# First attention of a two-layer encoder: PSUM copies at the end of a step, value products that wait by four key blocks, squares ahead of exponentials

## The reference, cut to what matters

```python
for qb in range(S // Q_BLOCK):                     # 8 blocks of 128 queries
    n_keys = q0 + Q_BLOCK                          # keys up to the block's end
    s = einsum('bqhcd,bkhcd->bhcqk', q[:, q0:n_keys], k[:, :n_keys]) * scale
    s = s + _rel_bias(q0, n_keys, rel_table)[None, :, None]
    p = _masked_softmax(s, _chunk_mask(q0, n_keys)[None, None, None])
    a = p[:, :, 0] - lam * p[:, :, 1]
    outs.append(einsum('bhqk,bkhe->bqhe', a, v[:, :n_keys]))
o = _rms_norm(concatenate(outs, axis=1), subln_w) * (1.0 - lam_init)
return o.reshape(B, S, D_MODEL) @ w_o
```

## Time and profile before

| | |
|---|---|
| median of the runs | 3080.66 us (3074.52, 3080.66, 3080.73) |
| the profiled execution | 3074.19 us, span of its records 3072.5 us |
| first attention in it | about 150 to 760 us |
| PE busy over the span | 2708.4 us (88%) |
| DVE, ACT, POOL busy | 1689.0 (55%), 1184.6 (39%), 336.0 us (11%) |

### The profile page before, as it was taken

The page is one execution under the profiler, slowest core; times in us unless marked ns, Lnnn a source line. Parts: engine busy times, 40 slices in busy tenths (PEclk is TensorE's granted clock), DMA queues, the critical chain, the costliest instruction groups (busy, mean ns, idle before and its releaser), DMA issues.

```text
span 3072.5 us, 37975 instructions
## 1 busy us (share of the span) xinstructions
PE 2708.4 (88%) x12716; PEld 2231.9 (73%) x12716; DVE 1689.0 (55%) x2888; ACT 1184.6 (39%) x2125; POOL 336.0 (11%) x362
## 2 busy tenths in 40 slices
PE   1678878887999999999998788888789999999996
PEld 1566666665778888888776677777567888888884
DVE  3466666665575444354375777777558323232346
ACT  0355555554262120312255565665426212131223
POOL 2000000000020001016032322222101000000000
PEclk9789998886999999999999999999899999999997
DMA  6422222223434324142233111111353211111122
GB/s 195 143 68 73 70 69 66 64 59 145 150 95 130 103 69 135 44 129 61 71 115 86 21 32 27 27 32 26 128 159 86 77 48 48 48 48 48 48 82 76
DMA packets 331200, 245.78 MB, mean 80 GB/s; under 512 B 41000, under 2 KB 303447, under 8 KB 331103
## 3 DMA queue, kind: packets, MB, share of 16 engines
q1 hardware_dynamic: 314062, 185.82, 20.7%
q0 software_dynamic: 17040, 58.73, 6.3%
HBM read 215.12 MB, written 33.59 MB: 81 GB/s over the span
## 4 chain that ended last, share of the span: by engine, by line
PE 63%; DVE 13%; ACT 10%; issue 9%; DMA 4%; ACTq 0%; DVEq 0%; POOL 0%; SPq 0%; POOLq 0%
PE PA L1651 31%; PE SC L1651 24%; PE VB L1739 3%; DVE H L1184 2%; DVE soft L1566 2%; ACT H L729 2%; ACT X L745 2%; DMA ada<-in_ada_w 1%; DVE W L1102 1%; ACT X L1028 1%; ACT W L683 1%; PE TB L1658 1%; DVE H L1223 1%; ACT H L723 1%; DVE X L1588 1%
## 5 line engine op out<-in xcount | busy, mean ns | idle before, releaser
L1651 PE MATMUL PA<-U,W 128*128 128x512 f32 x3840 | 948.8, 402 | 80.8 <-DVE W L1102 46.9
L1651 PEld LDWEIGHTS PA<-U,W 128*128 128x128 f32 x3840 | 730.6, 192 | 245.5 <-issue 57.7
L683 ACT ACTIVATE W<-raw 128x1024 fp32r<-128x1024 f32 (+2 forms) x262 | 259.8, 992 | 830.9 <-PE PA L1651 389.9
L1651 PE MATMUL SC<-U,W 128*128 128x512 f32 x2064 | 484.2, 394 | 4.4 <-DVE W L1102 4.2
L1651 PEld LDWEIGHTS SC<-U,W 128*128 128x128 f32 x2064 | 389.5, 189 | 91.5 <-DVE W L1102 5.9
L1102 DVE TENSOR_TENSOR W<-raw,W 128x1024 fp32r<-128x1024 f32 (+2 forms) x262 | 313.8, 1198 | 99.6 <-ACT W L683 97.9
L1651 PE MATMUL PA<-H,W 128*128 128x512 f32 x1536 | 358.7, 393 | 3.2 <-DVE W L1102 3.2
L1651 PE MATMUL SC<-H,W 128*128 128x512 f32 x1536 | 354.4, 390 | 0.0
L1651 PEld LDWEIGHTS PA<-H,W 128*128 128x128 f32 x1536 | 288.6, 189 | 64.3 <-DVE W L1102 3.6
L1651 PEld LDWEIGHTS SC<-H,W 128*128 128x128 f32 x1536 | 288.5, 188 | 60.5 <-issue 1.0
L729 ACT ACTIVATE H<-TB 128x512 fp32r<-128x512 f32 (+3 forms) x216 | 107.8, 499 | 217.0 <-PE TB L1658 215.6
(11 more groups left out here) (209 smaller groups left out, 2984.1 us busy)
## 6 DMA issues: line engine op xcount, KB each, us to landing
raw<-in_ffn_w SPq DMA_DIRECT2D x160, 512.0 KB, 4.1
ada<-in_ada_w POOLq DMA_DIRECT2D x96, 512.0 KB, 4.7
U<-attention_out SPq DMA_DIRECT2D x4, 3584.0 KB, 17.4
raw<-in_da_w_qkv SPq DMA_DIRECT2D x24, 512.0 KB, 4.2
attention_out<-ostage SPq DMA_DIRECT2D x32, 256.0 KB, 2.7
raw<-in_da_w_o SPq DMA_DIRECT2D x16, 512.0 KB, 4.1
X<-residual SPq DMA_DIRECT2D x4, 2048.0 KB, 11.6
attention_out<-ostage SPq DMA_DIRECT2D x64, 128.0 KB, 2.3
```

The costliest lines, as they stand in the source:

```text
L683: nc.scalar.activation(W[:, slot, 0, 0:kt * P], raw[:, slot, 0:kt * P], ACT.Copy).then_inc(w_hi, 1)
L1651: ins = mm(bank, W[:, slot, a, kt * P:(kt + 1) * P], moving(b, kt)[:, cols], start=kt == first and (a, b) == SPLIT[0], stop=kt == last and ...
```

## The change

There are three edits in the written order, and none of them adds arithmetic.

- On ACT, `copy_piece0` moves from just behind the exponentials to the end of the step, behind `scale0` and the reciprocal root. On DVE, `lo_piece0` moves behind the second evacuation group `a_lo(h, s-1, 1)`.
- On ACT, `out_square` moves ahead of the exponentials.
- On PE, `values0` waits before key block 0 for the evacuation of the blocks 0 to 3, and before key block 4 for that of the blocks 4 to 7, in place of one wait for the last group.

```diff
@@ ACT heads0
                         a_hi(h - 1, NQ - 1, 0)
+                    if square is not None:
+                        out_square(*square)
                     exps0(h, s)
-                    if s == 0 and not is_first(h):
-                        copy_piece0(p, h, LAST_PIECE)
-                    if proj and s in PIECE_DONE:
-                        copy_piece0(1 - p, h + 1, PIECE_DONE[s])
...
                     if store is not None:
                         out_hi(a0, store[0], store[1], P, ofin)
-                    if square is not None:
-                        out_square(*square)
                     scale0(h, s)
                     if square is not None:
                         rms_of_pair(*square)
+                    if s == 0 and not is_first(h):
+                        copy_piece0(p, h, LAST_PIECE)
+                    if proj and s in PIECE_DONE:
+                        copy_piece0(1 - p, h + 1, PIECE_DONE[s])
@@ DVE heads0
-                    if s == 0 and not is_first(h):
-                        lo_piece0(p, h, LAST_PIECE)
-                    if proj and s in PIECE_DONE and PIECE_DONE[s] // 2 != 1:
-                        lo_piece0(1 - p, h + 1, PIECE_DONE[s])
...
                         a_lo(h - 1, NQ - 1, 1)
+                    if s == 0 and not is_first(h):
+                        lo_piece0(p, h, LAST_PIECE)
+                    if proj and s in PIECE_DONE and PIECE_DONE[s] // 2 != 1:
+                        lo_piece0(1 - p, h + 1, PIECE_DONE[s])
@@ PE values0
-                pe.wait_ge(a0["t_evac"], 14 * h + group_of0(last, 1 if last >= 4 else 0) + 1)
                 for j in range(last + 1):
+                    if j % 4 == 0:
+                        pe.wait_ge(a0["t_evac"], 14 * h + group_of0(last, j // 4) + 1)
```

## The result

| | before | after |
|---|---|---|
| median of 20 runs each | 3074.05 us (3062.27 to 3086.77) | 3081.50 us (3078.38 to 3082.94) |
| profiled execution | 3074.19 us, span 3072.5 | 3080.43 us, span 3078.7 |
| ratio | | 1.0027, 95% interval 1.0017 to 1.0038 |

The change made the kernel slower by 0.27%. The forecast was 3080 us and "no change". The time lies 1.5 us beside it, but what it was to be compared with was 3074 and not the 3080.66 of the first three runs, and 0.27% is more than the 0.2% that I had called no change.

The account below looks back on a forecast made before the run. PE, the busiest engine, was seen held by waits and slow clock, within a step chain over DVE and ACT. Chain terms of -7.8 us plus 13.2 for the clock gave +5.4 on 3074.19: 3080 us, range 3064 to 3099.

Parts of the forecast that it names:

- no change: Whole kernel: the forecast itself, 3080 us, own range 3074 to 3087, called within 0.2% of before; chance 0.36.
- The named signs: First attention: value waits gone, L1223 and `max0` spacings, new PE waits in steps 1 and 7, heads of 76 to 79 us.
- step 1: Projection and `max0` start together, -3.3 us; with the earlier square -4.0 us a head, before the clock.
- the clock term in step 1: First half piece of the next projection, after PE's wait: low clock, 4.71 us against 3.02, +1.7 a head.
- its bound: Limits for the slowed half piece in step 1: 0 and 12 x 0.2 more matmul time, given as 2.3 us.
- The 4 us that I gave for it: Half piece of step 1 at half rate throughout, twice 12 x 0.24: total some 4 us higher.
- step 3: Scaling, root and copies in series add +2.8 us; slack of 1.5 before the exponentials is used up: net +1.3 a head.
- Step 7: Exponentials no longer behind an evacuation that waited for PE, -1.3 us; slowed second half piece, +0.5 a head.
- step 0: Copies come behind two evacuations, staging and scaling, partly offset by less waiting for PE's transposes: +0.4 us a head.
- PE takes the whole gain: Rival: DVE's step has room for the later copy, 13 us a head saved in seven heads, 2983 us; chance 0.05.
- The clock holds: Rival: PE's few instructions in the new gaps keep the clock up, the 13.2 us go, 3066 us; chance 0.25.
- The low clock spreads: Rival, steps 7 to 1: slow half pieces delay step 1's transposes, 4.0 us a head, 3090 to 3094 us; chance 0.34.

Follow-up runs that it names:

- e4: Early squares and split value wait put on the kernel before, without the late copies: ratio 0.9865, median 3029.7 us.
- e6: The full change, but ACT copies the q pieces (steps 6 and 0) early, right behind the exponentials: ratio 0.9969 to the kernel before, 3061.9 us.
- e7: The full change, but ACT copies the k pieces (steps 2, 3) early, and in fact the v pieces too: ratio 0.9937 to the kernel before, 3055.7 us.
- e9: The full change without the split wait (late copies and early squares): ratio 1.0038 to the kernel before, 3082.8 us.
- e5: The full change plus 16 overwritten filler matmuls on PE before step 1's wait for the weight slab: ratio 1.0011 to the kernel before, 3076.4 us.
- e1: Only the late copies and low parts, put on the kernel before; squares and value wait as before: ratio 1.0128, 3110.5 us.
- e10: The full change without the early squares (late copies and split wait): ratio 1.0114 to the kernel before, 3109.7 us.

## Why the prediction was wrong

**The mechanism held.** The named signs are in the profile after: of the waits before L1740 0.15 us is left; L1223 of step 6 3.41 us behind the difference (forecast about 3.4); `max0` of step 7 13.52 us behind that of step 6 (13.4); PE 4.93 us before the projection of step 1, released by DVE's W (3 to 5), and 4.10 before the scores of the next head (about 4). Heads 1, 2, 4, 5 and 6 last 78.3 to 79.3 us (76 to 79), and head 3 82.6, since DVE's pause at its end is now on the path in full (13.16 us for the 9.22 of step 7 elsewhere). e4, e6 and e7 show the cause by undoing it.

**The step that failed is the size of the clock term in step 1.** I put the slow half piece at 4.71 us, +1.7, from the nearest row, and gave 2.3 as its bound. It took 5.35 us here, and 5.17 to 5.49 in heads 1, 3, 5 and 6 as well; only in head 4 it was 4.60. The six together took 31.2 us, 2.9 more than six of 4.71. With that in place of the term, the sum is +8.3 us or 0.27%, which is not "no change". The granted clocks (the number before the last two) tell why the row was the wrong one. Shown are the row in the kernel before, the piece of head 4 in the kernel after, and a piece of e9 that had the low clock from end to end:

```profile
545.59:550.30 4.71, 4.71 (x17) 3.69 (x15) 2.73 (x9) 1.84 (x3) 0.00 (x0) 0.64 0.00 0
...
472.67:477.27 4.60, 4.60 (x14) 3.62 (x15) 1.95 (x10) 1.10 (x4) 0.00 (x0) 0.63 0.57 171
...
550.04:555.53 5.49, 5.49 (x13) 4.28 (x14) 1.95 (x10) 1.09 (x4) 0.00 (x0) 0.50 0.48 143
```

With 0.64 a part of the 4.71 ran at the full clock, while the piece of 5.35 us had 0.51 over its first 5.2 us. So that row was no measure of a piece that begins after a wait of 4.9 us, and the bound was the better value. The rule of the Trainium skill (TensorE: Matmul & The Clock Gate, Part 1) that I had set beside it, half rate when the recent past was idle, agrees with this piece. The 4 us that I gave for it go with the bound of 2.3, though; a piece of twice 12 x 0.24 is 5.76 us and would have added 6. e5 measures the term: with a full clock the piece takes 3.04 us and step 1 9.55 us, so -4.2 against before (counted -4.0), and the low clock costs 2.4 us of it.

The other terms of the sum, a head: step 3 +1.72 for +1.3, nearly as large a miss (2.6 us over six heads), because the slack of 1.5 us was not used up in full (the exponentials still started 0.3 us after the maxima were ready, behind evacuation and square) and the reciprocal root waited 0.35 us for PE's sum of squares. Step 7 has -1.28 with nothing for the clock, where I had added +0.5. The slow half piece is there (4.50 us at 374.67), but what waits for it is the transposes for step 0: they start at 379.00, 0.8 us after the end of the scaling (377.02 + 1.16). So the term belongs to step 0, which has +0.56 for +0.4. Ahead of heads 1, 2, 3, 5 and 6 this piece takes 4.98, 4.62, 4.50, 4.27 and 4.37 us, and their step 0 takes 10.69, 10.32, 10.23, 10.03 and 10.10: always 5.7 us more than the piece.

In sum head 2 grew by 3.55 us for 2.8, and the six heads from head 1 to head 7 by 475.7 - 463.2 = +12.5 us for +7.8. Head 0 gave +4.3 (counted +4.2), the last head, up to the projection behind it, about -7.9 for -6.6. So in the first attention +8.9 us stand against a sum of +5.4. In the profiled executions the span grew by 6.2 us only; some 1.4 us were won ahead of the first attention and 1.2 behind it, with which the change has nothing to do.

**The comparison was wrong as well.** The sum of +5.4 us is 0.18%, just inside the 0.2% of no change, and I then set the 3080 us beside a median of three runs, two of which (3080.7) lay in the upper quarter of what this kernel does (3062 to 3087 in 20 runs). With 3074 as its base, which the profiled execution had shown, the same sum stood at the edge between same and slower. The medians differ by 7.4 us, 2 more than the sum, and that is over the edge. The chances had stood at 0.36 for no change and 0.34 for slower, so the call was a narrow one. That the 3080 us fell so close to the measured 3081.5 is in part luck: misses of both signs, inside the first attention and outside it, nearly cancel.

**The rivals.** "PE takes the whole gain" (2983) needed a way around scaling, copy and `max0`; there was none in this kernel. "The clock holds" (3066) is what e5 built on purpose for step 1 alone, and it came to 3076: the half piece of step 7 stayed slow (4.2 to 4.9 us), the filler cost head 0 2.5 us, and three heads had a slow piece in step 5 instead. "The low clock spreads" (3090 to 3094) did not come about in the kernel after, since the early square keeps PE ahead; in e1 and e10, which lack it, it did, with 3110 us. There the place was the square of step 7 and the transposes of step 0, and not those of step 1 as I had put it.

## What to carry to other kernels

When a wait of the busiest engine is to be removed by moving work on the others, follow the longest in-order chain of those others from one iteration's mark to the next, and write down for each step what is beside it and what is in series; here this walk gave every step to 0.6 us, where the list of waits promised 13 us a head. A copy that lies under another engine's computation is free only there: moved by one place, from beside DVE's difference to behind ACT's scaling, two kinds of copies cost 1.6% together, more than the two good edits brought. Test the edits of a bundle singly, and take the base of a 0.2% question from as many runs as the question needs.

## What the runs showed of the hardware

A wait of PE does not by its length alone decide what the work behind it costs. In e1 and in e9 (the same kernel but for the squares) PE waits exactly 3.48 us for the slab in step 1, behind the same products. In e1 the half piece then took 5.48 us; in e9, in head 3, it took 3.01, and in head 5 of the same execution, behind the same 3.48 us, 5.49:

```profile
383.74 3.05 PE L1739 MATMUL VB<-H 128*128 128x256 f32 x24 [1.41 <-DVE H L1184]
386.63 0.30 PE L1658 MATMUL TB<-cst,X 128*128 128x128 f32 x1
390.41 3.01 PE L1651 MATMUL PA<-U,W 128*128 128x512 f32 x12 [3.48 <-DVE W L1102]
...
425.48 4.58 PE L1651 MATMUL PA<-U,W 128*128 128x512 f32 x12
...
550.04 5.49 PE L1651 MATMUL PA<-U,W 128*128 128x512 f32 x12 [3.48 <-DVE W L1102]
```

In e9 step 1 lasted 9.6 us in heads 3, 4 and 6 and 12.0 to 12.3 in heads 1, 2 and 5 (in head 4 PE waited 1.21 us only; in the others 3.3 to 3.5). So one program, in one execution, pays the 2.4 us in some heads and not in others. Not all of it is saved: in just the heads 3, 4 and 6 a half piece of step 5 is slow (4.58 us at 425.48), and steps 5 and 6 together take 22.3 us instead of 21.3.

I had not expected that the kernel after is so much steadier than the one before (its 20 runs lie within 4.6 us, those of before within 24.5 us); the one has the low clock at the same place in nearly every head, the other changes between 75.2 and 78.6 us a head. That this is what spreads the runs is an inference from one profile each and was not tested. A part of the spread lies elsewhere: from the last value product to the end of the span the code is the same in all fourteen kernels, and in their profiled executions it took between 2311.3 and 2317.5 us.
